# Hybrid decoder layer with expert retrieval: every eighth v row of chunks 1 to 7 goes to VectorE's side sum

## What is computed

```python
experts = jnp.take_along_axis(cidx, pos, axis=-1)      # 8 heads x 16 experts per token
gates = jax.nn.softmax(top_s, axis=-1)
u_sel = u_tab[experts]
act = jax.nn.gelu(jnp.einsum('chkd,cd->chk', u_sel, xc))
w = gates * act
v_sel = v_tab[experts]
return jnp.einsum('chk,chkd->cd', w, v_sel)            # y; the layer returns h + y
```

## Time and profile before

| | us |
|---|---|
| median of three runs | 2968.72 |
| the profiled execution | 2962.76 |
| its span, first to last instruction | 2961.0 |
| TensorE busy (matmuls) | 2598.8 (88%) |
| VectorE busy | 2109.0 (71%) |
| GpSimd busy | 1988.3 (67%) |
| ScalarE busy | 869.9 (29%) |
| DMA | 1125.71 MB, mean 380 GB/s |

### The profile page before, as it was taken

The page is one execution under the profiler, slowest core; times in us unless marked ns, Lnnn a source line. Parts: engine busy times, 40 slices in busy tenths (PEclk is TensorE's granted clock), DMA queues, the critical chain, the costliest instruction groups (busy, mean ns, idle before and its releaser), DMA issues.

```text
span 2961.0 us, 29850 instructions
## 1 busy us (share of the span) xinstructions
PE 2598.8 (88%) x7593; PEld 1178.0 (40%) x7593; DVE 2109.0 (71%) x5265; ACT 869.9 (29%) x2022; POOL 1988.3 (67%) x2061
## 2 busy tenths in 40 slices
PE   8999758878988999798988999799988999777778
PEld 4454324433442445244433445244533445222223
DVE  2878648986787778877787778877787767754443
ACT  3322233134212422145213532255213532111111
POOL 1004447777777777777777777777777777777775
PEclk9999979999999999999999999999999999999999
DMA  7127879999999999999999999999999999999999
GB/s 251 33 79 270 332 284 417 382 390 418 419 419 420 416 418 419 403 415 411 419 419 413 402 418 419 407 405 406 419 419 399 379 419 419 415 420 419 420 419 358
DMA packets 321506, 1125.71 MB, mean 380 GB/s; under 512 B 36481, under 2 KB 44697, under 8 KB 321336
## 3 DMA queue, kind: packets, MB, share of 16 engines
q0 software_dynamic: 294912, 1073.87, 90.1%
q1 hardware_dynamic: 26424, 49.92, 4.6%
HBM read 1115.20 MB, written 8.45 MB: 379 GB/s over the span
## 4 chain that ended last, share of the span: by engine, by line
PE 26%; DMA 21%; issue 19%; POOL 16%; DVE 4%; ACT 2%; POOLq 0%; ACTq 0%; DVEq 0%
PE psum L1548 18%; POOL w_kept L1451 9%; DMA ring_v<-in_peer_v,experts 9%; DMA w_kept<-in_peer_u,experts 9%; POOL ring_v L1451 6%; PE psum L1011 2%; PE psum L1482 2%; DMA w_kept<-in_peer_v,experts 1%; DVE w_kept L1864 1%; PE psum L990 1%; PE psum L1508 1%; DMA qT<-qT_spill 1%; PE psum L1498 1%; DVE top_v L1120 0%; ACT L1684 0%
## 5 line engine op out<-in xcount | busy, mean ns | idle before, releaser
L1548 PE MATMUL psum<-ring_v,diag 128*128 128x512 f32 x3372 | 1629.2, 609 | 257.8 <-DMA ring_v<-in_peer_v,experts 165.6
L1864 DVE CUSTOM_DVE_ANT_0 w_kept<-w_kept,psum 128x1024 f32<-128x1024 f32 x960 | 1164.7, 1218 | 541.2 <-DMA w_kept<-in_peer_u,experts 538.1
L1451 POOL DMA_INDIRECT w_kept<-in_peer_u,experts x954 | 920.4, 965 | 311.0 <-issue 239.5
L1451 POOL DMA_INDIRECT ring_v<-in_peer_v,experts x878 | 850.9, 969 | 324.2 <-issue 242.7
L1548 PEld LDWEIGHTS psum<-ring_v,diag 128*128 128x128 f32 x3372 | 591.1, 191 | 1065.3 <-issue 791.7
L1693 ACT ACTIVATE diag<-ident,weights 128x128 f32<-128x128 f32 x983 | 355.0, 393 | 739.7 <-PE psum L1548 583.5
L1548 PE MATMUL psum<-w_kept,diag 128*128 128x512 f32 x560 | 270.1, 605 | 41.6 <-DMA w_kept<-in_peer_v,experts 30.5
L513 PE MATMUL psum<-w_sb,xnT 128*128 128x512 f32 x640 | 281.7, 598 | 0.0
L466 POOL DMA_INDIRECT w_kept<-in_peer_u,experts x70 | 65.7, 939 | 278.6 <-DVE experts L1271 230.7
L1820 DVE SCALAR_TENSOR_TENSOR acc<-conv_in,taps,acc 128x128 f32<-128x128 f32 x720 | 205.0, 347 | 0.1
L513 PEld LDWEIGHTS psum<-w_sb,xnT 128*128 128x128 f32 x640 | 121.1, 192 | 145.3 <-issue 140.4
(11 more groups left out here) (229 smaller groups left out, 1747.0 us busy)
## 6 DMA issues: line engine op xcount, KB each, us to landing
w_kept<-in_peer_u,experts POOLq DMA_INDIRECT x1024, 10.0
ring_v<-in_peer_v,experts POOLq DMA_INDIRECT x878, 10.0
w_sb<-in_w_in SPq DMA_DIRECT2D x4, 2048.0 KB, 19.6
x_in<-in_x SPq DMA_DIRECT2D x8, 512.0 KB, 8.6
w_kept<-in_w_out SPq DMA_DIRECT2D x1, 4096.0 KB, 13.3
h_res<-in_x SPq DMA_DIRECT2D x8, 512.0 KB, 6.8
w_kept<-in_peer_wq SPq DMA_DIRECT2D x1, 4096.0 KB, 12.5
wo_sb<-in_w_out SPq DMA_DIRECT2D x1, 4096.0 KB, 17.9
```

The source lines that it names most:

```text
L1451: nc.gpsimd.indirect_dma_start(slot(kind, n), None, peer_u[0] if kind == "u" else peer_v[0], bass.IndirectOffsetOnAxis(S.experts[c % 2][:, ...
L1548: last = nc.tensor.matmul(y_ps[:, j * BANK:(j + 1) * BANK], diag[:, e % DIAGS, :], slot("v", n)[:, j * BANK:(j + 1) * BANK], start=e == 0, ...
L1864: nc.vector.tensor_tensor_reduce(out=row, in0=row, in1=hn, scale=1.0, scalar=0.0, op0=ALU.mult, op1=ALU.add, accum_out=dots[:, e:e + 1]).t ...
```

## The change

SIDE also lists rows e = 6, 14, ..., 102 of each of chunks 1 to 7: 13 rows a chunk, 91 in all. VectorE adds them to y_side as in chunk 0. The first of a chunk starts the sum anew, with a multiplication alone, once the copy of the chunk before is done. copy_y of ScalarE is gone; VectorE's end_first_y becomes end_y_of(c) for chunks 0 to 6 and adds y_side to y_ps at the same slot. In chunk 7 the five side rows of the tail continue the chunk's sum.

```diff
     SIDE = ([row_of(FIRST, e) for e in range(CAUGHT) if e % 3 == 2]
+            + [row_of(c, e) for c in range(FIRST + 1, CHUNKS) for e in range(ROWS - LAG) if e % 8 == 6]
             + [row_of(TAIL, e) for e in range(ROWS - LAG, ROWS) if e % 4 == 3])
-    FIRST_SIDES = len([n for n in SIDE if n < ROWS])
+
+    def sides_before(c):
+
+        return len([n for n in SIDE if n < ROWS * c])
...
-            def copy_y(c):
-                act.wait_ge(S.taken, c + 2)
-                for j in range(2):
-                    at = slice(j * BANK, (j + 1) * BANK)
-                    if j == 0:
-                        act.wait_ge(half_added, c + 1)
-                    else:
-                        act.wait_ge(row_added, pe_rows(ROWS * (c + 1) - 1))
-                    nc.scalar.activation(y_out[:, at], y_ps[:, at], ACT.Copy).then_inc(y_copied, 1)
...
-                        if s == LAG and c > FIRST + 1:
-                            copy_y(c - 1)
...
-                if n in (0, FIRST_SIDES):
+                if n == sides_before(at // ROWS):
+                    if at >= ROWS:
+                        dve.wait_ge(y_copied, 2 * (at // ROWS))
                     nc.vector.tensor_scalar(y_side, row, weights[:, e:e + 1], None, ALU.mult).then_inc(side_added, 1)
...
-            def end_first_y():
-
-                dve.wait_ge(S.taken, FIRST + 2)
-                dve.wait_ge(side_added, FIRST_SIDES)
+            def end_y_of(c):
+
+                dve.wait_ge(S.taken, c + 2)
+                dve.wait_ge(side_added, sides_before(c + 1))
                 for j in range(2):
                     at = slice(j * BANK, (j + 1) * BANK)
                     if j == 0:
-                        dve.wait_ge(half_added, FIRST + 1)
+                        dve.wait_ge(half_added, c + 1)
                     else:
-                        dve.wait_ge(row_added, pe_rows(ROWS - 1))
+                        dve.wait_ge(row_added, pe_rows(ROWS * (c + 1) - 1))
                     nc.vector.tensor_tensor(y_out[:, at], y_ps[:, at], y_side[:, at], ALU.add).then_inc(y_copied, 1)
...
-                        if c == FIRST and v is not None and in_side(*v):
+                        if v is not None and in_side(*v):
                             add_row_aside(SIDE.index(row_of(*v)))
-                        if c == FIRST + 1 and s == LAG:
-                            end_first_y()
+                        if s == LAG and c > FIRST:
+                            end_y_of(c - 1)
...
-            for n in range(FIRST_SIDES, len(SIDE)):
+            for n in [SIDE.index(t) for t in SIDE if t >= row_of(TAIL, ROWS - LAG)]:
                 add_row_aside(n)
```

## The result

The changed kernel takes 2974.41 us, the median of 15 runs (2970.88 to 2980.51), where the kernel before takes 2966.85 in 15 runs of the same sessions. The ratio is 1.0028, 95% interval 1.0020 to 1.0036: slower by 8.3 us (5.9 to 10.7), a third of the 24.8 us forecast. The profiled execution took 2973.8 us.

The account below looks back on a forecast made before the run. GpSimd's gather issue was taken as the bound, transfers 1 to 2% slower. 3 x 4.7 + 7.0 + 1 + 2.7 = 24.8 us on the profiled 2962.8, and 6.0 to the median, gave 2993 us (2967 to 3016).

Parts of the forecast that it names:

- Who paces the kernel: Chunks 1 to 7: GpSimd issues a gather every 1.24 us and sets the pace, transfers 1 to 2% slower.
- the stretched gather: GpSimd: a gather starting inside a VectorE side addition is held until it ends, 0.36 us per addition (0.22 to 0.53).
- I charge half: Chunks 2 to 4: with a backlog of transfers, half of each chunk's holding counts, 3 x 2.35 = 7.0 us.
- chunk 1's full 4.7 us: Chunk 1: starts with landing at 6.6 us, no backlog, so its holding of 13 x 0.36 us counts in full.
- Chunks 5 and 6: Both run their backlog down already: holding of 4.7 us each in full, plus 1.37 us each for the copy.
- Chunk 7: A backlog of 4.5 us would grow here; GpSimd 4.7 us later uses that up, leaving a cost of 1 us.
- The copy: Result copy moved to VectorE at slot 20: nothing in chunks 1 to 4, 2.7 us in 5 and 6; bounds 0, 8.2.
- TensorE's relief: 91 rows off TensorE, 178 us of its busy time, priced at nothing because GpSimd's pace covers it.
- the transfers absorb it: Rival: a chunk's transfers need 325 to 328 us whatever GpSimd does; costs 0 to 6 us, chance 0.12.
- a faster kernel, by TensorE's relief: Rival: three rows per chunk leave attention, 5.9 us of TensorE's time, so scans come sooner; 2951 at best, chance 0.09.
- a much slower one, with VectorE as the bound: Rival: VectorE's 17 us per chunk fall where it lacks slack; +121 if all exposed, half +60, chance 0.07.
- the forecast's small end: Holding of 0.22 us per addition, 2.9 a chunk, chunks 2 to 4 and 7 absorbing theirs, copy at nothing: +9 us.

Follow-up runs that it names:

- z_two_sbuf: Kernel before plus 91 extra VectorE additions with both operands in SBUF, all rows kept on TensorE: 2978.55 us, ratio 1.0042.
- z_one_psum: Kernel before plus the same 91 extra VectorE additions with the second operand in PSUM: 2970.10 us, ratio 1.0009.
- the held gathers alone: Kernel before plus z_two_sbuf's extra additions in some chunks only: chunks 1 to 4 (52) 2971.91 us, chunks 5 and 6 (26) 2974.22 us.
- y_side7: Kernel before with the change in chunk 7 alone, unchanged up to the end of chunk 6: 2966.16 us, ratio 0.9999.

## Why the prediction was off

**Who paces the kernel, and the stretched gather: right.** 0.36 us per addition was the term; the change shows 31.8 / 91 = 0.35 of the page's busy time (29.6 / 91 = 0.33 by the gathers inside additions alone, where chunk 0 before has 13.8 us for 35 additions, 0.39), every fourth row 0.35, the pure pair 0.28. That the holding costs more than VectorE's time is shown by the pair of z_two_sbuf and z_one_psum. The Trainium skill's inference (page "SBUF — State Buffer", section "Who interferes with whom") that such an instruction leaves descriptor generation alone would have had the gathers unstretched; the measurement decides against it, with 25.9 us over 91 additions.

**The step that failed: "I charge half", and with it chunk 1's full 4.7 us.** Chunks 1 to 4 were charged 11.7 us. In the change's profile they are 1.5 us longer, the change in them alone measures +2.7, the held gathers alone +4.2. I had read the earlier trace rows rightly (about 16 us of waits for dots net of the ordinary 0.30) and used it only for a rival. It is the very quantity that tells how much can be absorbed: those waits come from late landings, and in the change's profile 11.6 us of them are gone. I had charged the holding against the length of the backlog, when it had to be charged against GpSimd's waits as well. With the held gathers alone, 16 of 23 us of holding in these chunks came back. In chunk 1, which I took to start without a backlog, one grows within the chunk (the median landing from 700 to 950 us was 10.6 us before), so it too could give.

**Chunks 5 and 6: half right.** 4.7 + 1.37 us each were charged; the profile shows +4.2 and +3.8. That this lies near the holding by itself is in part luck. By the profiles, the two chunks together are 6.5 us longer than before with the held gathers alone, 5.1 longer with the copy alone (665.4 us), and 3.1 shorter with the rows dropped (657.2): 8.5 in sum, against the change's 8.0. Each is one profile, and y_side7, unchanged there, took 658.6 where before took 660.3, so each term may be off by some 2 us. Alone, the change in them measured +3.0, with relief and copy in it, and the held gathers alone +6.2.

**Chunk 7: right in kind.** Charged 1 us; measured -0.3, with landing at 8.8 us in place of 12.0, the backlog used up as the text had it. GpSimd was held there for 2.5 us and not 4.7.

**The copy: the size is not refuted.** 2.7 us were charged, +2.4 measured, in an interval from -0.6 to +5.0 that reaches zero. The place was right: in that kernel's profile chunks 5 and 6 are 2.5 and 2.6 us longer, chunks 1 to 4 within 0.2. So was the wait: TensorE waited 11.8 us in seven waits for the copy in the changed kernel, 6.6 in six before; chunk 0's form, which the prediction had as free of waits, was 0.6 us of these. In the changed kernel (first) TensorE's row 0 of chunk 3 waits for VectorE, then runs slowly; before (second) it waited for ScalarE:

```profile
1345.64 2.77 PE L1552 MATMUL psum<-w_kept,diag 128*128 128x512 f32 x4 [2.64 <-DVE hn_next L1895]
1348.21 1.06 PE L1502 MATMUL psum<-ident,relu_z 128*128 128x128 f32 x4
1349.07 2.38 PE L1552 MATMUL psum<-ring_v,diag 128*128 128x512 f32 x4
```

```profile
1338.29 1.96 PE L1548 MATMUL psum<-w_kept,diag 128*128 128x512 f32 x4 [1.01 <-ACT hn_next L1704]
1340.08 0.60 PE L1498 MATMUL psum<-ident,relu_z 128*128 128x128 f32 x4
1340.52 1.88 PE L1548 MATMUL psum<-ring_v,diag 128*128 128x512 f32 x4
```

**TensorE's relief: priced at nothing, measured -2.1 us**, with no change inside its interval. Its busy time fell less than forecast, which the last section takes up. In chunks 5 and 6 it may be worth more: there the change alone measured less than the held gathers alone.

The parts add up to 12.5 - 2.1 + 2.4 = 12.8 us, and the change measures 8.3. The interval of the first part alone is 8 us wide, so the sum does not contradict the result; and the extra additions held GpSimd more than the change's did (35.4 against 29.6 us). Whether relief is worth more once gathers are held was not tried and stays open.

The rivals: "the transfers absorb it" was nearest to the truth in kind, though not complete, since 8.3 us is beyond what a measurement can tell from no change. Neither a faster kernel, by TensorE's relief, nor a much slower one, with VectorE as the bound, appeared. The measured time lies in the stated range, between the absorption case (0 to 6 us, chance 0.12) and the forecast's small end (+9); the range's upper end, 3016, is 3017 by its own sum.

## What to carry to other kernels

When a change delays an engine that issues transfers, first find out how much that engine already waits, directly or through another engine, for transfers it issued itself. Net of the ordinary gap, that wait is a budget that pays for new delay, and a second dose of the same work finds it spent (here 91 additions cost 8 us and the next 98 cost 28). And an instruction should be costed by where its operands lie: 91 instructions of 1.28 us on VectorE cost 12.5 us of time with both operands in SBUF and 2.7 with one in PSUM.

## What had not been expected of the hardware

TensorE's granted clock fell after it was left waiting. Around row 0 of chunk 3 in the changed kernel:

```profile
1340.00:1345.60 5.60, 3.00 (x7) 0.81 (x5) 5.57 (x12) 1.80 (x6) 4.10 (x5) 1.00 1.03 416
1345.60:1348.00 2.40, 2.35 (x4) 0.98 (x5) 2.40 (x4) 0.00 (x0) 1.87 (x2) 0.72 1.02 413
1348.00:1350.00 2.00, 2.00 (x7) 1.26 (x6) 0.37 (x2) 0.69 (x3) 1.59 (x2) 0.50 1.03 422
1350.00:1354.00 4.00, 4.00 (x18) 2.44 (x17) 2.60 (x5) 3.94 (x12) 3.08 (x4) 0.99 1.03 420
```

After 2.64 us of waiting for VectorE's copy the clock is granted at 0.72 and then 0.50 (1.2 in place of 2.4 GHz), and is back at 0.99 in the stretch from 1350 us on; the four matmuls of a row take 2.77 and 2.38 us where they take 1.96 and 1.88 after a wait of 1.01, at a granted clock of 1.00 throughout. A slower clock may also eat into relief. With 91 rows dropped, TensorE's page says

```profile
PE 2494.6 (84%) x7229; PEld 1142.0 (39%) x7229; DVE 2109.6 (71%) x5265; ACT 836.6 (28%) x1931; POOL 1994.9 (67%) x2061
```

2494.6 us busy for 364 matmuls fewer: 104 us less than before, not 178, at a mean granted clock of 0.961 in place of 0.986. Here, with work taken off the engine, the rest of its work ran slower.

The second surprise is the chips. The same kernel before takes 2966 to 2968 us on three of the chips used and 3343 on one, where the transfers run at some 355 GB/s. What a change costs can depend on that: the additions with two operands in SBUF cost +12.5 us (8.3 to 16.3) on the one and +6 (0.7 to 12.0) on the other, intervals that still overlap.
